# A two-block network on one core: the second block's first projection in three rounded products instead of one fp32 product, with the norm applied after the products

## What is computed

```
x = x + expert_choice_moe(...)            # end of the first block
x = rms_norm(x, final_g)                  # the first block's output
h = _rmsnorm(x, g_mix); proj = h @ w_in   # 1024 x 5648
(gq, gk, gv, gz, gbeta, galpha, mq, mk, mv, mo, mi, mf, gate_a, gate_b) = split(proj)
qkv = silu(causal_conv([gq, gk, gv], conv_w))
o_a = gated_delta_rule(l2norm(gq), l2norm(gk), gv, g, beta)
y_a = (head_rmsnorm(o_a) * silu(gz)) @ w_branch_a
o_b = mlstm_chunkwise(mq, mk, mv, mi, mf)
y_b = (head_rmsnorm(o_b) * sigmoid(mo)) @ w_branch_b
x = x + (sigmoid(gate_a) * y_a + sigmoid(gate_b) * y_b) @ w_out
```

## Time and profile before

| | |
|---|---|
| median of 3 runs | 2354.06 us (2350.6 to 2356.39) |
| the profiled execution's own time | 2353.52 us |
| its span in the trace | 2351.7 us |
| PE busy | 2143.3 us (91%) |
| DVE busy | 621.4 us (26%) |
| ACT busy | 498.9 us (21%) |

### The profile page before, as it was taken

One profiled execution on the slowest core, in us unless ns is written; L12 is line 12 of the kernel. 1 busy time (PEld: TensorE's weight loads), 2 busy tenths in 40 slices (PEclk: granted clock), 3 DMA queues, 4 the chain that ended last, 5 costly groups with the idle time before them and its releaser, 6 DMA issues.

```text
span 2351.7 us, 21421 instructions
## 1 busy us (share of the span) xinstructions
PE 2143.3 (91%) x8814; PEld 1200.6 (51%) x8814; DVE 621.4 (26%) x905; ACT 498.9 (21%) x782; POOL 109.7 (5%) x119
## 2 busy tenths in 40 slices
PE   6999959989999999899996999999999989999998
PEld 5766433323333333333332535566556768887866
DVE  4634130100101011000102237311345342224224
ACT  4124120000000000000002223231232232223134
POOL 2420000000000000000000000220000000000000
PEclk9999979999999999999998899999999989999998
DMA  9310619999999999999996120010112212123230
GB/s 239 130 63 2 250 72 393 428 428 428 429 428 428 428 428 428 429 429 429 428 427 259 36 72 36 36 54 19 54 54 87 75 53 107 72 107 114 103 105 36
DMA packets 45902, 507.04 MB, mean 216 GB/s; under 512 B 6528, under 2 KB 6656, under 8 KB 10512
## 3 DMA queue, kind: packets, MB, share of 16 engines
q1 hardware_dynamic: 43408, 499.54, 52.1%
q0 software_dynamic: 2432, 6.61, 1.2%
HBM read 504.00 MB, written 2.10 MB: 215 GB/s over the span
## 4 chain that ended last, share of the span: by engine, by line
PE 73%; DMA 20%; DVE 3%; ACT 3%; issue 1%; POOL 0%; SPq 0%; ACTq 0%; DVEq 0%
DMA arena<-in_w_gu_dram 19%; PE bank L1941 11%; PE bank L1963 5%; PE bank L640 5%; PE bank L522 4%; PE bank L783 4%; PE bank L784 4%; PE bank L785 3%; PE bank L547 3%; PE bank L1909 3%; PE bank L1810 2%; PE bank L808 2%; PE bank L809 2%; PE bank L810 2%; PE bank L1926 2%; PE bank L1670 1%
## 5 line engine op out<-in xcount | busy, mean ns | idle before, releaser
L1941 PE MATMUL bank<-arena 128*64 128x512 f32 x2048 | 487.0, 632 | 79.1 <-DMA arena<-in_w_gu_dram 78.3
L1941 PEld LDWEIGHTS bank<-arena 128*64 128x64 f32 x2048 | 163.6, 145 | 372.7 <-issue 371.7
L1963 PE MATMUL bank<-arena 128*64 128x512 f32 x1024 | 232.3, 594 | 0.7 <-ACT arena L2528 0.6
L2321 DVE TENSOR_TENSOR arena<-arena,bank 128x256 f32<-128x256 f32 x64 | 27.0, 421 | 691.3 <-ACT arena L2524 691.3
L1963 PEld LDWEIGHTS bank<-arena 128*64 128x64 f32 x1024 | 76.3, 137 | 141.2 <-issue 141.2
L783 PE MATMUL bank<-input_rounded,weight_rest 128*128 128x512 f32 x352 | 141.1, 401 | 4.9 <-DVE weight_rest L1123 4.9
L2524 ACT ACTIVATE arena<-bank 128x256 f32<-128x256 f32 x64 | 24.6, 384 | 561.5 <-PE bank L1941 561.5
L784 PE MATMUL bank<-input_rest,weight_rounded 128*128 128x512 f32 x352 | 141.1, 401 | 0.0
L785 PE MATMUL bank<-input_rounded,weight_rounded 128*128 128x512 f32 x352 | 138.9, 395 | 0.0
L640 PE MATMUL bank<-arena 128*128 128x512 f32 x256 | 113.5, 595 | 0.0
L547 PE MATMUL bank<-arena 128*128 128x512 f32 x192 | 87.1, 604 | 0.0
(11 more groups left out here) (432 smaller groups left out, 2740.3 us busy)
## 6 DMA issues: line engine op xcount, KB each, us to landing
arena<-in_w_gu_dram SPq DMA_DIRECT2D x128, 2048.0 KB, 28.5
arena<-in_w_d_dram SPq DMA_DIRECT2D x64, 2048.0 KB, 25.2
arena<-in_wpack_dram SPq DMA_DIRECT2D x82, 1024.0 KB, 4.8
arena<-in_x_dram SPq DMA_DIRECT2D x2, 2048.0 KB, 8.8
arena<-in_xT_dram SPq DMA_DIRECT2D x2, 1024.0 KB, 6.8
out_dram<-arena SPq DMA_DIRECT2D x4, 512.0 KB, 2.6
arena<-in_rpbw_dram POOLq DMA_DIRECT2D x16, 96.0 KB, 28.1
arena<-in_wpack_dram SPq DMA_DIRECT2D x2, 512.0 KB, 7.8
```

What stands on the lines that cost most here:

```text
L1941: last = mm(ab[64 * x:64 * x + 64, :], xsT[:, k, 64 * x:64 * x + 64], w[x][:, k, :], start=k == 0, stop=k == KD - 1)
L1963: last = mm(bank[4 + n][64 * x:64 * x + 64, :], hidT[c % 2][:, P * t + 64 * x:P * t + 64 * x + 64], w[:, x, t, 512 * n:512 * n + 512], sta ...
```

## The change

Every product of the second block's first projection is now made of three rounded products. The weights come as **units** of 128 columns (half a slot of the ring): 4 units of q, a unit of the sixteen gate columns padded with zeros to 128, 8 more of q, k and v, 4 for mv, 12 for mq, mk, gz and mo, 16 for the branch gates, 45 in all (`N_UNITS`). `round_unit(j)` on ScalarE makes the rounded copy into one of two buffers, once unit j-2 is done; `rest_unit(j)` on VectorE makes the rest; `unit_products` on PE uses them in 24 matmuls.

x is no longer normalised before the product. `turn_tile` turns the raw `x_res` between the last scatter's matmuls into all eight banks; ScalarE and VectorE write rounded x and its rest straight from these, scaled by the product of both gains (`gcol`). The factor of both norms for each token is worked out beside the first units, broadcast over the partitions by four matmuls into `rrow`, and VectorE multiplies every finished bank by it (`q_scaled`, `aside_scale`, `gate_scale`); for mv it is the scale of ScalarE's copy. gz and mo are kept turned and gate the heads' outputs after their turn (`turned_gated`), no longer before it. The residual x (first norm applied) goes to DRAM (`x_kept`, four stores of 512 KB) and is loaded back with one DMA before the output projection.

```diff
+            def unit_products(j, b, ks=range(KD)):
+                if ks[0] == 0:
+                    pe.wait_ge(S("ulo_made"), j + 1)
+                for k in ks:
+                    mm(b, wl[:, k, :], hhi[k], start=k == 0, stop=False)
+                    mm(b, wh[:, k, :], chlo[k], start=False, stop=False)
+                    last = mm(b, wh[:, k, :], hhi[k], start=False, stop=k == KD - 1)
+                if ks[-1] == KD - 1:
+                    last.then_inc(S("unit_done"), 1)
...
+            first_pair()
+            unit_products(2, bank[2][:, :])
+            pe.wait_ge(S("r_made"), 1)
...
+            unit_products(3, bank[3][:, :])
+            unit_products(U_GATES, bank[5][:, :])
+            for u in range(4, N_QKV):
+                pe.wait_ge(S("cv_done"), nth("cv_done", u - 3))
+                unit_products(qkv_unit(u), bank[u % 4][:, :])
...
+            def rest_unit(j):
+                if j < N_UNITS:
+                    dve.wait_ge(S("uhi_made"), j + 1)
+                    tt(out=unit_lo(j), in0=unit_raw(j), in1=unit_hi[j % 2], op=ALU.subtract).then_inc(S("ulo_made"), 1)
...
+                dve.wait_ge(S("unit_done"), qkv_unit(u) + 1)
+                tt(out=ps[:, :], in0=ps[:, :], in1=rrow, op=ALU.mult).then_inc(S("q_scaled"), 1)
+                if u >= 2:
+                    rest_unit(qkv_unit(u) + 2)
...
                 dve.engine_nop().then_inc(S("prep_done"), 1)
+                for v in ((0, 1), (2, 3), (4,), (5,))[n]:
+                    aside_scale(v)
...
+            def round_unit(j):
...
+                    act.wait_ge(S("unit_done"), j - 1)
+                fn(unit_hi[j % 2], unit_raw(j), ACT.Copy).then_inc(S("uhi_made"), 1)
...
             def gate_out(f):
-                act.wait_ge(S("sg_filled"), f + 1)
-                fn(sg[f], b[:, :], ACT.Sigmoid).then_inc(S("sg_made"), 1)
+                round_unit(U_SG + f + 2)
+                act.wait_ge(S("sg_scaled"), f + 1)
+                fn(sg[f], sg[f], ACT.Sigmoid).then_inc(S("sg_made"), 1)
...
-            scatter(NP, range(8))
+            for i in range(NT):
+                scatter(NP, (2 * i, 2 * i + 1))
+                if i:
+                    pe.wait_ge(S("sc_added"), 8 * (NP - 1) + 2 * (i - 1) + 4)
+                    turn_tile(i - 1, range(6))
```

More of the change, by code:

```diff
@@ L65 @@
 N_CHUNKS = C_PG + N_PG
+C_FIRST = N_CHUNKS
 NSLOT = 8
@@ L334, in program @@
             used[C_OUT1 + i] = ("out1_filled", 4 * (i // 2 + 1))
[L335 to L342, removed]
+        for i in range(N_RING):
+            used[C_RING + i] = ("unit_done", min(U_RING + 2 * i + 2, N_UNITS))
         for i in range(N_BR):
@@ L477, in norm_scale @@
                     .then_inc(S("norm_scaled"), 1)
-        def norm_turn_dve(dve, norm, gain):
-            for k in range(1, KD, 2):
-                dve.wait_ge(S("norm_turned"), KD * (norm - N3) + k + 1)
-                dve.tensor_scalar(hT[:, k, :], bank[7][:, :], col(gain, k), None, ALU.mult).then_inc(S("norm_tv"), 1)
         def hv(v, h):
@@ new lines, in aside @@
+                unit_products(U_ASIDE + v, bank[6 + v % 2][:, :], range(4 * half, 4 * half + 4))
+            first_pair()
+            unit_products(2, bank[2][:, :])
+            pe.wait_ge(S("r_made"), 1)
+            for i in range(NT):
+                last = mm(bank[7][:, P * i:P * i + P], r13[:, i:i + 1].to_broadcast([P, P]), ident, start=True, stop=True)
+            last.then_inc(S("rrow_filled"), 1)
+            unit_products(3, bank[3][:, :])
+            unit_products(U_GATES, bank[5][:, :])
@@ new lines, in second_pe @@
+            for u in range(4, N_QKV):
+                pe.wait_ge(S("cv_done"), nth("cv_done", u - 3))
+                unit_products(qkv_unit(u), bank[u % 4][:, :])
+                if u == 4:
+                    pe.wait_ge(S("gates_copied"), nth("gates_copied", 1))
+                    for i in range(NT):
+                        last = turn(bank[6][:, 16 * i:16 * i + 16], gT[0:16, P * i:P * i + P], ident[0:16, 0:16])
+                    last.then_inc(S("gates_filled"), 1)
+            pe.wait_ge(S("gg_made"), 2)
@@ L878, in second_dve @@
-            g3 = bank[0][:, 0:64].rearrange("p (i g) -> p i g", g=16)
+            stt(out=r13, in0=s3, scalar=1.0 / D, in1=veps, op0=ALU.mult, op1=ALU.add).then_inc(S("norm_var"), NT)
+            dve.wait_ge(S("norm_sd"), NT)
+            dve.reciprocal(r_both, r_both).then_inc(S("r_made"), 1)
+            dve.wait_ge(S("r_made"), 1)
+            rest_unit(2)
+            rest_unit(3)
+            dve.wait_ge(S("rrow_filled"), 1)
+            own(dve.tensor_copy(rrow, bank[7][:, :]))
+            own.wait()
@@ L1093, in second_dve @@
                 mix_tile(2 * i + 1)
-            for u in range(4, 8):
-                turned_rest(u)
+            turned(1)
             branch_rest(3)
```

522 lines of the change are left out of this document (313 added, 209 removed), and 2 rows, old and new, of the table at.

## The result

The changed kernel took 2314.03 us (median of 4 runs, 2311.64 to 2316.87) beside 2353.57 us for the kernel before (4 runs): a ratio of 0.9833, 95% interval 0.9816 to 0.985, a gain of 39.5 us. The time lies inside the forecast range, 15 us over the forecast value. A second set of 5 runs gave 2317.81 us and 0.9848 (0.9833 to 0.9863).

What follows compares the result with a forecast made beforehand. TensorE was taken to bound most of the second block's first half, except at the seam and in l2 and prep. Stage gains summed to 54.3 us off the profiled 2353.5, giving 2299 us, range 2277 to 2323.

Steps and rivals of the forecast that it cites:

- The likeliest case, the sum with its chains: Whole kernel: stage gains add up with the engines' chains as laid out, 2285 to 2313 us; chance 0.62.
- The third case, a slow start: Seam: first pair and unit 2 run at 1.2 GHz throughout, similar loss at restarts, 2312 to 2325 us; chance 0.18.
- A product, a unit.: TensorE: a unit of 24 rounded products takes 5.5 us, bounds 5.44 and 5.68, and saves 1.4; half a unit 0.69.
- Seam and qkv, 26.4: Last scatter add to the end of qkv: 93 us instead of 119.4, with 6 for slow clock; gain 26.4.
- the rule on transposes that I set beside it: Seam: transposes don't count as activity that raises the clock, so the first pair runs at 1.2 GHz whatever precedes it.
- l2, -0.5: l2: VectorE's chain sets the time and TensorE hides in it, 46 us against 45.5; loss 0.5.
- prep, 6.8: prep: shorter chunks and an estimated 4.2 less from chunk 3 to the first correction, 65.1 us against 71.9; gain 6.8.
- inverse, 8.3: Inverse: 12 halves lie on TensorE's path, each saving 0.69 us; gain 8.3.
- recurrence, 5.5: Recurrence: 8 halves lie on TensorE's path, each saving 0.69 us; gain 5.5.
- mLSTM, 4.8: mLSTM: first head stays at 19.4 us, a head otherwise takes 17.5, stage 80.9 of 85.7; gain 4.8.
- branches, 3: Branches: three units save 4.2 us and a 2 us rounding wait goes, less longer waits and 1 of clock; gain 3.
- Stores and load of x at nothing: DMA of x: stores and the load back cost nothing; if either were late, some 9 us.

Runs made afterwards that it cites:

- `later_order`: Changed kernel with unit 17's rest earlier in l2, the w stage waiting for one factor fewer, and turned slices gated earlier in the branches: 2303.36 us.
- `seam_order`: Changed kernel with the seam reordered: TensorE finishes unit 0 before unit 1, and roundings and rests of units 2 and 4 come earlier: 2305.26 us.
- `mlstm_order`: Changed kernel with three mLSTM moves: row maxima before gate bank 3's factor, gz's silu later, later heads' exponential before the gate bank's sigmoid: 2308.27 us.
- `best_order`: Changed kernel with all the earlier order moves joined, plus further ones at the seam and in the first mLSTM head: 2276.15 us.
- `fill_order`: `best_order` with unit 23 computed right behind prep's third-chunk half, where TensorE waits, leaving the inverse loop ten halves instead of twelve: 2271.71 us.

## Why the prediction held, and where its terms were off

The likeliest case, the sum with its chains, came true as a mechanism: waits for a rest at units 2, the gates' and 19 (2.8, 4.4 and 3.5 us against 3, 4.8 and 3.7), none in most units. The third case, a slow start, did not: the first pair ran at full clock. The sum was 15 us too high: 11.7 of it lie in the stages below, 2.6 in the stretch ahead of the scatter, which the change does not touch. Every stage but the first came out below its forecast, and the seam's 2.3 us more hid a part of that. That the time fell inside the range is owed to the range's width as well as to the sum.

- **A product, a unit.** 0.235 us apart, 5.6 a unit, at the upper end of my bounds: 4 us over 44 units. Rounding 1.05 and rest 1.24 us on average, as taken from the rows.
- **Seam and qkv, 26.4.** 28.7. Start and both waits cost less clock than the 6 us that I added: the two restarts 1.4 and 2.4, the first pair nothing. By the rule on transposes that I set beside it (the Trainium skill, TensorE: Matmul & The Clock Gate, section "Part 4: PE-mode transpose") the pair would have run at 1.2 GHz; it ran at 2.4 GHz, after 32 turns in one block too. And the 0.65 that I read for the turns of before was a mean of 0.51 and 1.00: the clock rose within them.
- **l2, -0.5.** -1.3 between the two profiles, up to 2.8 us worse in other executions of the same instructions. I said that TensorE hides in VectorE's time, and missed that unit 17's rest stands behind a reciprocal of 3.35 us; `later_order` gives 1.8 us back, and without that wait l2 took 38.2 us in all three profiles.
- **prep, 6.8. This term failed.** 1.6. Of the five missing, 4.6 are the step "its halves end early now and no longer stand ahead of the turns", my estimate of 4.2: from VectorE's last product of chunk 3 to the first product of two masks and turns, the trace of before has 11.8 us and the changed one 12.3, all of it GpSimd's masks, VectorE's subtractions, turns and copies handing two buffers around; TensorE's halves held it for 0.5 us at most. I had taken the difference of two stage lengths for a stall and had no row of one. Chunk 0 took 18.1: my 16.4 and the 1.6 for the half clock behind its wait, as forecast.
- **inverse, 8.3.** 5.3. A half saves 0.62, not 0.69 (7.4 in all), and the w stage got a wait of 1.5 for the last factor, which I had not followed past the last correction. The first half saved nothing: from the first correction to the turn behind it both traces have 4.55 us, the changed one with 1.9 us at 0.51 left over from the waits ahead.
- **recurrence, 5.5.** 5.0, except where the clock falls (0 then).
- **mLSTM, 4.8.** 2.6. The later heads, 17.7, are the forecast's 17.5, with its order of exponential and sigmoid. In the first head I had unit 5 start 2.8 us late; where the clock held it started 3.0 us late and the head took 21.8. Mis-sized were TensorE's own part (17.07 for my 16.6) and the clock: 22.4 in this profile, for my 19.4 and 1.6 of clock.
- **branches, 3.** 0.7. The first turned slices wait behind gate bank 12's factor and rest (2.2 us and half clock), and 3.3 us stand between the branches; `later_order` wins 7.6 of it.
- **Stores and load of x at nothing:** no wait for either shows in any profile.

## What to carry to other kernels

When a matmul is split into rounded terms, look less at how long a rounding and a rest take than at what stands ahead of them in a queue at the stage's edges. Here 35 us more came from order alone (38 between the medians, 2314 to 2276), with every instruction kept, and 4 more from putting a ready unit into a gap. Before a stall is booked as gain, find the row in which the engine waits for the thing that gets cheaper: a difference of two stage lengths is no such row. And where the next wait will be when this one is gone can often be read in the same trace: `seam_order` met one at unit 6, `mlstm_order` one at the differences.

## What the runs showed of the hardware

- **The clock after a wait differs between executions of the same instructions.** After l2's wait of 6.8 us, the same in all ten profiles, the granted clock stayed at 0.5 for between 2.8 and 6.2 us. Of the shorter waits some were followed by half clock in one execution and not in the next: 2.19 us at the turned slices in 5 profiles of 6; 1.5 in the w stage in 2 of 7; 2.98 in the output projection in 8 of 10, while in `later_order` and `seam_order` the clock stayed at 1.00 behind it. A wait of 2.1 ahead of unit 17 left the clock up, one of 2.12 ahead of prep in the kernel before did not. The first mLSTM head's small turns, broadcast and scores lost the clock without a wait in `best_order` and kept it in `fill_order`. A fall costs 1.3 to 5 us. No run here shows what decides.
- **VectorE and GpSimd take turns** when both read two operands from SBUF: beside a mask a rest took 1.91 us instead of 1.22, a subtraction 1.74 instead of 0.68, and beside a rest a mask took 2.24 instead of 1.26.
- **Turns keep the clock, and it can rise in them.** 3.8 us of nothing but 128x128 turns, behind a busy scatter, left it at 1.00, and it stayed there for the first pair. Before the change it rose from 0.51 to 1.00 within the turns, and fell again in products of 128x16 with TensorE busy throughout.
